# The last expert item: rows back to the tokens by one-hot matmuls, the other items' rows loaded while it runs

## What is computed

```python
def moe_swiglu(h, w_router, b_router, w_gate, w_up, w_down):
    ...
    logits = (t @ w_router).astype(jnp.float32)
    _, top_idx = lax.top_k(logits + b_router.astype(jnp.float32), TOP_K)      # 2 of 8 experts
    top_w = jax.nn.softmax(jnp.take_along_axis(logits, top_idx, axis=-1), axis=-1)
    gates = jnp.sum(jax.nn.one_hot(top_idx, N_EXPERTS) * top_w[..., None], axis=1)
    for e in range(N_EXPERTS):
        out = out + gates[:, e:e + 1] * swiglu(t, w_gate[e], w_up[e], w_down[e])  # 1024 -> 2816 -> 1024
...
y = rmsnorm(x + moe_swiglu(...), g_final)
```

## Time and profile before

| what | value |
|---|---|
| median of 3 runs | 1471.12 us (1465.41 to 1472.30) |
| profiled execution | 1469.05 us |
| its span, first to last instruction | 1467.2 us |
| mean granted TensorE clock | 0.965 of full speed |
| busy share: TensorE, VectorE, ScalarE, GpSimd | 94%, 64%, 52%, 5% |
| last matmul starts at | 1438.25 us of the span |

### The profile page before, as it was taken

One profiled execution on the slowest core, in us unless ns is written; L12 is line 12 of the kernel. 1 busy time (PEld: TensorE's weight loads), 2 busy tenths in 40 slices (PEclk: granted clock), 3 DMA queues, 4 the chain that ended last, 5 costly groups with the idle time before them and its releaser, 6 DMA issues.

```text
span 1467.2 us, 19059 instructions
## 1 busy us (share of the span) xinstructions
PE 1375.5 (94%) x6832; PEld 1109.2 (76%) x6832; DVE 933.8 (64%) x880; ACT 769.3 (52%) x742; POOL 73.7 (5%) x103
## 2 busy tenths in 40 slices
PE   4899999989989999968999999999999999999982
PEld 4789999877666555546888888888888888888871
DVE  2534343355445222237788888888888888888883
ACT  1433233334344222125777777777777777777761
POOL 1000000002100000000001001010010010100001
PEclk9899999999979999978999999999999999999996
DMA  8543443230212221276899999999999999999934
GB/s 260 187 157 106 167 130 127 79 132 11 65 35 84 84 65 45 78 288 258 324 365 366 399 362 378 380 362 395 360 371 386 373 385 364 373 391 362 382 116 125
DMA packets 136562, 354.98 MB, mean 242 GB/s; under 512 B 18282, under 2 KB 54458, under 8 KB 136177
## 3 DMA queue, kind: packets, MB, share of 16 engines
q1 hardware_dynamic: 133337, 343.73, 64.8%
q0 software_dynamic: 3184, 10.71, 1.9%
HBM read 346.74 MB, written 7.82 MB: 242 GB/s over the span
## 4 chain that ended last, share of the span: by engine, by line
PE 92%; DVE 3%; ACT 2%; DMA 1%; issue 1%; POOL 1%; SPq 0%; ACTq 0%; DVEq 0%; POOLq 0%
PE PS L1411 24%; PE PS L1413 23%; PE PS L1412 23%; PE PS L1684 3%; PE PS L1715 2%; PE PS L1752 2%; PE PS L1613 2%; PE PS L1717 1%; PE PS L1816 1%; PE PS L1425 1%; PE PS L1436 1%; PE PS L1577 1%; PE PS L1664 1%; PE PS L1587 1%; PE PS L1809 1%
## 5 line engine op out<-in xcount | busy, mean ns | idle before, releaser
L955 DVE TENSOR_TENSOR LOW<-RAW,UH 128x2048 fp32r<-128x2048 f32 x275 | 628.0, 2291 | 154.6 <-ACT UH L669 154.6
L669 ACT CAST UH<-RAW 128x2048 fp32r<-128x2048 f32 x275 | 526.1, 1914 | 253.5 <-PE PS L1413 253.5
L1411 PE MATMUL PS<-UH,XH 128*128 128x512 f32 (+1 forms) x768 | 292.5, 381 | 1.4 <-DVE XL L1308 1.4
L1412 PE MATMUL PS<-LOW,XH 128*128 128x512 f32 (+1 forms) x768 | 290.5, 378 | 0.0
L1413 PE MATMUL PS<-UH,XL 128*128 128x512 f32 (+1 forms) x768 | 290.5, 378 | 0.0
L1411 PEld LDWEIGHTS PS<-UH,XH 128*128 128x128 f32 x768 | 145.2, 189 | 30.5 <-DVE XL L1308 1.8
L1413 PEld LDWEIGHTS PS<-UH,XL 128*128 128x128 f32 x768 | 145.4, 189 | 29.3
L1412 PEld LDWEIGHTS PS<-LOW,XH 128*128 128x128 f32 x768 | 145.3, 189 | 28.5
L1411 PE MATMUL PS<-UH,ATH 128*128 128x512 f32 x352 | 138.4, 393 | 4.7 <-DVE ATL L1324 4.7
L1413 PE MATMUL PS<-UH,ATL 128*128 128x512 f32 x352 | 137.8, 392 | 0.0
L1412 PE MATMUL PS<-LOW,ATH 128*128 128x512 f32 x352 | 137.7, 391 | 0.0
(11 more groups left out here) (256 smaller groups left out, 1557.8 us busy)
## 6 DMA issues: line engine op xcount, KB each, us to landing
RAW<-in_moe_w_down SPq DMA_DIRECT2D x88, 1024.0 KB, 5.4
RAW<-in_moe_w_gate SPq DMA_DIRECT2D x64, 1024.0 KB, 5.1
RAW<-in_moe_w_up SPq DMA_DIRECT2D x64, 1024.0 KB, 5.1
RAW<-in_moe_w_gate SPq DMA_DIRECT2D x24, 768.0 KB, 6.5
RAW<-in_moe_w_up SPq DMA_DIRECT2D x24, 768.0 KB, 7.1
PAIR<-in_ffn_w_gate SPq DMA_DIRECT2D x11, 1024.0 KB, 5.2
PAIR<-in_ffn_w_up SPq DMA_DIRECT2D x11, 1024.0 KB, 7.8
RAW<-in_ffn_w_down SPq DMA_DIRECT2D x11, 1024.0 KB, 5.0
```

Source lines behind the costliest of these rows:

```text
L669: nc.scalar.copy(dst, src).then_inc(unit_high, 1)
L955: V_.tensor_tensor(dst, src, high.bitcast(F32), ALU.subtract).then_inc(unit_low, 1)
L1411: mm(out, wh, xh, start=start, stop=False, skip_group_check=True)
L1412: mm(out, wh, xl, start=False, stop=False, skip_group_check=True)
```

## The change

The rows of the last item no longer go through DRAM. Three one-hot tiles (BACK, slots x tokens of one tile) are made from the last item's column of IDX; the result is split into a high part (YH) and a low part (YL), and matmuls with BACK bring each row to its token, in free PSUM banks. VectorE adds them with the token's weight for that item (`RC[:, 4]`). The rows of the other items are loaded from YD as soon as ring slots 0 to 2 are free, and added with weights that are zero where a row belongs to the last item. As such rows in YD are now never written by an item, YD is filled with finite numbers early in the program. The last item's down of block 2 runs one output half after the other, and the turn of its hidden block stands one unit earlier. Empty slots now point at an extra row 0 of the tokens' buffer HND, so that they match no token. The table "items" is replaced by the start of "iota", and three semaphores of the gains become one.

```diff
+YG_FREE = next(i for i in range(len(LAST) - RING, len(LAST)) if (NF + i) % RING == 0) + 1   # 15
 ...
-    put("tokens", np.stack([token, token, 2 * token + 1, 2 * token + 2], 1))
+    put("tokens", np.stack([token + 1, token + 1, 2 * token + 1, 2 * token + 2], 1))
 ...
+    BACK = place("BACK", [P, NT, TT], F32R, XN_OFF)
+    YH = place("YH", [P, D], F32R, FFN_OFF + 3 * 4 * UNIT)
+    YL = place("YL", [P, D], F32R, FFN_OFF + 3 * 4 * UNIT + 4 * D)
 ...  SP
-        sp.wait_ge(y_last, 16)
         for t in range(NT):
+            sp.wait_ge(unit_used, NU * (before_last + 1) + NF + YG_FREE + t)
             rows = YD[1 + 2 * t * TT:1 + 2 * (t + 1) * TT, :].rearrange("(p i) d -> p (i d)", i=2)
             sp.dma_start(YG[t][:, :, :].rearrange("p i d -> p (i d)"), rows).then_inc(y_in[t], 16)
 ...  POOL, after the roots of the first dense layer
+        for t in range(NT):
+            pool.wait_ge(normed[1], t + 1)
+            for i in range(2):
+                store(YD[1 + 2 * t * TT:1 + 2 * (t + 1) * TT, :].rearrange("(p i) d -> p i d", i=2)[:, i, :], HN[:, t, :])
 ...
-                    pool.dma_start(HND[MIXED[k] * TT:(MIXED[k] + 1) * TT, :], HN[:, MIXED[k], :]).then_inc(y_stored, 16)
+                    if k == 0:
+                        pool.dma_start(HND[0:1, :], HN[0:1, MIXED[0], :]).then_inc(y_stored, 16)
+                    pool.dma_start(HND[1 + MIXED[k] * TT:1 + (MIXED[k] + 1) * TT, :], HN[:, MIXED[k], :]).then_inc(y_stored, 16)
 ...
+        nc.gpsimd.tensor_copy(IDXL[:, :], IDX[:, 0, :][:, bass.ds(before_last, 1)]).then_inc(back_ready, 1)
 ...  POOL, after the loop: the last item's scatter goes
-        pool.wait_ge(y_stored, 16 * before_last + 16 * NT)
-        pool.wait_ge(i_y, 2 * before_last + 4)
-        nc.gpsimd.tensor_copy(IDXY[:, :], IDX[:, 1, :][:, bass.ds(before_last, 1)]).then_inc(pool_step, 1)
-        steps[0] += 1
-        pool.wait_ge(pool_step, steps[0])
-        pool.indirect_dma_start(YD, bass.IndirectOffsetOnAxis(IDXY[:, 0:1], 0), YS[:, :], None).then_inc(y_last, 16)
 ...  ACT, item
+                if last and i == DN0:
+                    act.wait_ge(y_stored, 16 * j + 16 * (NT + 1))
 ...
-                elif i == GU0 - 1:
+                elif i == (GU0 - 2 if last else GU0 - 1):
                     hidden_high(2, j)
 ...
+            if last:
+                for h in range(2):
+                    act.wait_ge(unit_used, NU * (j + 1) + NF + len(order) - 2 + 2 * h)
+                    nc.scalar.copy(YH[:, h * 512:(h + 1) * 512], PS[:, 4 + h, :]).then_inc(i_y, 1)
+                return
 ...  DVE, before the second layer's first norm
+        dve.wait_ge(stored, 16 * (1 + 2 * NT))
 ...  DVE, item: hidden_low(2, j) moves as hidden_high does; after the last item
+        dve.wait_ge(back_ready, 1)
+        for t in range(NT):
+            V_.tensor_scalar(BACK[:, t, :], cn("iota")[:, 0:TT], float(1 + t * TT), IDXL[:, 0:1], ALU.add, ALU.is_equal)\
+              .then_inc(back_ready, 1)
         dve.wait_ge(r_act, 1)
         link(V_.tensor_tensor(rc(10), rc(6), rc(7), ALU.add))
         link(V_.reciprocal(rc(11), rc(10)))
         link(V_.tensor_tensor(RC[:, 6:8, :], RC[:, 6:8, :], RC[:, 11:12, :].to_broadcast([TT, 2, NT]), ALU.mult))
-        dve.wait_ge(gain4_in, 16)
+        link(V_.tensor_scalar(RC[:, 8:10, :].rearrange("p i t -> p (i t)"), SB[:, 0, :], TO[0:TT, 1, NE - 1:NE], -1.0,
+                              ALU.subtract, ALU.is_equal))
+        link(V_.tensor_tensor(RC[:, 0:2, :], RC[:, 6:8, :], RC[:, 8:10, :], ALU.mult))
+        link(V_.tensor_tensor(RC[:, 2:4, :], RC[:, 6:8, :], RC[:, 0:2, :], ALU.subtract))
+        link(V_.tensor_tensor(rc(4), rc(0), rc(1), ALU.add))
+        for t in range(NT):
+            dve.wait_ge(y_in[t], 16)
+            for i in range(2):
+                link(V_.scalar_tensor_tensor(out=X[:, t, :], in0=YG[t][:, i, :], scalar=RC[:, 2 + i, t:t + 1], in1=X[:, t, :],
+                                             op0=ALU.mult, op1=ALU.add))
+        for h in range(2):
+            dve.wait_ge(i_y, 2 * before_last + 3 + h)
+            cols = slice(h * 512, h * 512 + 512)
+            V_.tensor_tensor(YL[:, cols], PS[:, 4 + h, :], YH[:, cols].bitcast(F32), ALU.subtract).then_inc(back_ready, 1)
+        dve.wait_ge(later_gain_in, 48)
 
         def add_rows(t):
-            dve.wait_ge(y_in[t], 16)
-            link(V_.scalar_tensor_tensor(out=X[:, t, :], in0=YG[t][:, 0, :], scalar=RC[:, 6, t:t + 1], in1=X[:, t, :],
-                                         op0=ALU.mult, op1=ALU.add))
-            V_.scalar_tensor_tensor(out=X[:, t, :], in0=YG[t][:, 1, :], scalar=RC[:, 7, t:t + 1], in1=X[:, t, :],
-                                    op0=ALU.mult, op1=ALU.add).then_inc(x_added, 1)
+            dve.wait_ge(back_mm, t + 1)
+            V_.scalar_tensor_tensor(out=X[:, t, :], in0=PS[0:TT, back_bank(t):back_bank(t) + 2, :].rearrange("p b n -> p (b n)"),
+                                    scalar=RC[:, 4, t:t + 1], in1=X[:, t, :], op0=ALU.mult, op1=ALU.add).then_inc(x_added, 1)
 ...  PE, item
-            units(j, order, DN1, GU0)
+            units(j, order, DN1, GU0 - 1 if last else GU0)
 ...
             turn_hidden(2, j)
+            units(j, order, GU0 - 1 if last else GU0, DN2 if not last else GU0)
+            pe.wait_ge(i_atl, 6 * j + 6)
 ...
+            pe.wait_ge(unit_low, NU * (j + 1) + NF + len(LAST))
+            for h in range(2):
+                for q in range(3):
+                    slot, high = (NF + GU0 + q) % RING, (NF + GU0 + q) % HIGH
+                    for i in range(2):
+                        cols = slice((2 * i + h) * 512, (2 * i + h + 1) * 512)
+                        ins = three(PS[:, 4 + h, :], ATH[:, 2 * q + i, :], ATL[:, 2 * q + i, :], UH[high][:, cols],
+                                    LOWS[slot][:, cols], False, q == 2 and i == 1)
+                ins.then_inc(unit_used, 1 + h)
 ...  PE, after the last item
+        pe.wait_ge(back_ready, 1 + NT)
+        for t in range(NT):
+            for h in range(2):
+                if t == 0:
+                    pe.wait_ge(back_ready, 1 + NT + h + 1)
+                cols = slice(h * 512, h * 512 + 512)
+                mm(PS[0:TT, back_bank(t) + h, :], BACK[:, t, :], YH[:, cols], start=True, stop=False, skip_group_check=True)
+                ins = mm(PS[0:TT, back_bank(t) + h, :], BACK[:, t, :], YL[:, cols], start=False, stop=True, skip_group_check=True)
+            ins.then_inc(back_mm, 1)
+def back_bank(t):
+    return (0, 2, 6)[t]
```

More of the change, by code:

```diff
@@ L112, in landed @@
     return every, here + (1 if slot < NF else 0)
+YG_FREE = next(i for i in range(len(LAST) - RING, len(LAST)) if (NF + i) % RING == 0) + 1
+assert YG_FREE + 4 <= len(LAST)
 KB = [(0, 128), (128, 128), (256, 16)]
@@ L125 @@
 _W = [("ident", 128), ("upper", TT), ("iota", 128), ("part", 1), ("mask", 2 * P), ("maskt", TP), ("maskd", NS),
-      ("cos", NT * HALF), ("sin", NT * HALF), ("ridx", NE), ("tri", NE * NE), ("steps", NE * NT), ("items", MAXI), ("slots", MAXI + 2), ("tokens", 4 * NT)]
+      ("cos", NT * HALF), ("sin", NT * HALF), ("ridx", NE), ("tri", NE * NE), ("steps", NE * NT), ("slots", MAXI + 2), ("tokens", 4 * NT)]
 _WP = [("pm0", 4 * P), ("pm1", 4 * P), ("pstate", 4 * SMP)]
@@ L162, in shape_constants @@
     put("steps", np.tile(steps.reshape(1, -1), (P, 1)))
-    put("items", np.tile(np.arange(MAXI), (P, 1)))
     put("slots", np.tile(CAP * np.arange(MAXI + 2), (P, 1)))
     token = TT * np.arange(NT)[None] + np.arange(P)[:, None]
-    put("tokens", np.stack([token, token, 2 * token + 1, 2 * token + 2], 1))
+    put("tokens", np.stack([token + 1, token + 1, 2 * token + 1, 2 * token + 2], 1))
     def band(a, b, w):
@@ L319, in program @@
     EG = get("EG", [P, 1024])
+    XN_OFF = get.cur[0]
     XN = get("XN", [P, D])
@@ L363, in program @@
     x_in, consts_in, gains_in = sem("x_in"), sem("consts_in"), sem("gains_in")
-    gain1_in, gain4_in, small_in = sem("gain1_in"), sem("gain4_in"), sem("small_in")
-    gain3_in, dense_done = sem("gain3_in"), sem("dense_done")
+    later_gain_in, small_in = sem("later_gain_in"), sem("small_in")
+    dense_done = sem("dense_done")
     gain0_in, pool_in, pool_w_in = sem("gain0_in"), sem("pool_in"), sem("pool_w_in")
@@ L420, in program @@
         sem(n) for n in ("i_idx", "i_ix", "i_iy", "i_xn", "i_xt", "i_xh", "i_xl", "i_sg", "i_a", "i_t", "i_ath", "i_atl", "i_y", "y_stored"))
-    y_last = sem("y_last")
+    back_ready, back_mm = sem("back_ready"), sem("back_mm")
     y_in = [sem(f"y_in{t}") for t in range(NT)]
@@ L490, in _ @@
         sp.wait_ge(x_pooled, NT)
-        sp.dma_start(G[0][:, :], a["g_mix"][1:2, :].partition_broadcast(TT)).then_inc(gain1_in, 16)
+        sp.dma_start(G[0][:, :], a["g_mix"][1:2, :].partition_broadcast(TT)).then_inc(later_gain_in, 16)
         for c in range(RING_D, NC):
@@ L642, in _ @@
             pool.indirect_dma_start(XN[:, :], None, HND[:, :], bass.IndirectOffsetOnAxis(IDXC[:, 0:1], 0)).then_inc(i_xn, 16)
```

(20 more changed lines are left out.)

11 lines of the change are left out of this document (6 added, 5 removed).

## The result

| | before | after |
|---|---|---|
| median | 1471.12 us (1465.41 to 1472.30, 3 runs) | 1459.27 us (1457.84 to 1460.88, 4 runs) |
| profiled execution | 1469.05 us | 1457.84 us |
| its span | 1467.2 us | 1456.2 us |
| first to last index copy of the loop (six items) | 569.67 us | 570.72 us |
| last index copy to the end of the span | 103.67 us | 91.35 us |

The ratio of the mean times is 0.993, with an interval of 0.9906 to 0.9955: faster by 7 to 14 us. The median of 1459.27 lies within the 1450 to 1463 that was predicted, 2.8 above the 1456.5 named. The upper end of the interval lies just short of the 0.5% that can be told from no change. One disturbed run of the kernel before (1769.95) is left out.

A forecast was written before the change was run, and what follows sets the result against it. Bound taken: the 28.5 us tail after the last matmul, each step waiting for the previous. Savings of 5.3 (copy, scatter), 6.0 (load), 0.2 (stop) and 2.1 (adds) make 13.6: span 1453.6, predicted time 1456.5, range 1450 to 1463.

The forecast's parts named there:

- Scatter and load leave the path: In the tail: copy and scatter of the last item's rows save 5.3 us, the load of expert rows 6.0.
- The loads are hidden: Other items' rows, loaded after units 14 to 16, land by about 1419 us, 11 us before they are needed.
- The start of the down: The last down projection starts at 1428.36 us instead of 1428.60, a gain of 0.24.
- The 10.06 us of the down: The last down's 36 matmuls take 10.06 us as before, with the same loss of clock, ending at 1438.42.
- VectorE's new work: Under the last down: one-hot tiles 0.85 us, small operations 1.4, six adds 7.9, ending at 1438.4, tied with TensorE.
- The add out of PSUM: One add per tile in the tail, read from PSUM, takes 1.28 us, as the add of before.
- The root: GpSimd's root ahead of the first normalisation takes 0.9 us; 2.5 if slowness came from first use.
- At no cost: Six early 448 KB stores, the extra token row, index column copy, constants and merged semaphores add no time.
- Half clock to the end: Rival: TensorE stays at half clock from the last down to its end; 1461.7 to 1463.8 us, chance 0.09.
- Loads not hidden: Rival: other items' rows land only after the last down; gain only 1 to 2 us, 1468, chance 0.05.
- VectorE late: Rival: dearer VectorE work under the last down plus a slow root cost 3 to 4 us, 1460; within the main case.
- Starved dense steps: Rival: early stores hold back the first dense steps' weights, lasting until about 83 us at worst; slower, chance 0.03.

The follow-up runs named there:

- late_loads: Changed kernel with the loads of the other items' rows issued after the last down projection; last index copy to end 107.2 us, against 91.35 in the changed kernel.
- filled_stop: Changed kernel with 36 unneeded turns of the identity on TensorE in the stop ahead of the last down; last index copy to end 90.0 us, against 91.35.
- after_old_addresses: Changed kernel with 13 unused columns in the constants, so later tiles lie where they did before; median 1457.25 us, ratio to the kernel before 0.9906.
- stores_four_times: Changed kernel with the early stores into the expert rows made four times (24 instead of 6); span 1456.8 us, against 1456.2.
- tail_reordered: Changed kernel with old addresses, waits per unit, small operations ahead of the loop, reordered adds, back matmuls by halves; median 1451.54 us, ratio to the kernel before 0.9884.
- wait_per_unit: Changed kernel whose last down's first half waits for each weight unit's low part alone; median 1458.33 us, ratio to the kernel before 0.9934.

## Why the prediction was right, step by step

**Scatter and load leave the path: right.** The add of the first tile starts 2.2 us after the last down matmul, and no DMA stands in the chain until the outputs.

**The loads are hidden: right.** Landed by about 1418.5 (forecast 1419); late_loads shows what the cover is worth, 15.8 us.

**The start of the down: right.** 1429.65, where 1428.36 was forecast. The cast of unit 23 before it is already 1.39 late (1421.98 instead of 1420.59); without that the forecast is met to 0.1. The turn now takes place at 1421.78, between the two units.

**The 10.06 us of the down: mis-sized.** It was taken over from before, "the same loss of clock"; 13 slow matmuls instead of 9 made it 11.25, 1.2 more. That a stop costs the clock was right, as filled_stop shows; but a granted clock of 0.5 beyond the first nine matmuls is one of the prediction's own signs of being wrong, and the six adds end 1.5 us ahead of the last down matmul, not within the microsecond that it asked for. With the old addresses the down takes 10.12 (after_old_addresses), so the term was carried over from one set of addresses to another; what joins addresses and clock stays open.

**VectorE's new work: right.** One-hot tiles 0.65 instead of 0.85, small operations and adds as forecast; the adds end at 1439.43, and 1438.4 with the delay of 1.39 is 1439.8. The forecast named the tie as its weakest number, rightly: either engine alone gives 0 to 1.35 us, both 2.8. That a clock that does not fall would give nothing holds only where the two tie: it gave 1.35 in filled_stop, and after_old_addresses, whose down takes 10.12, ends as early as filled_stop (90.1 and 90.0).

**The add out of PSUM: right.** 1.28, as an add with both inputs in SBUF (1.28, L1405). The fixed part that the Trainium skill states as larger out of PSUM (VectorE: DVE Perf Modes, the section on the TRN2 errata) isn't seen in these rows.

**The root: right.** 0.9 and not 2.5. The second pair shows the reason: 1.06 where it starts under a normalisation, which reads two tensors in SBUF (1446.60 to 1447.88), and 0.57 for the next operation under the add out of PSUM; in tail_reordered 1.20 under an add of two SBUF inputs (1442.39 to 1443.67), after 73 us without work. That is the lock of the Trainium skill (SBUF — State Buffer, section "SBUF: two separate sides"); all rows here agree, and the rival of first use falls.

**"At no cost": wrong in one word, the constants.** The stores cost nothing, as stores_four_times shows. But the constants without the table of items move every tile behind them by 64 bytes, and the items become 0.17 us longer, 1.05 between the copies. The 1.2 us of the down go with the same addresses. The prediction counted the instructions of that edit and not the addresses.

So 1.39 us upstream (1.05 in the loop by the addresses, 0.27 ahead of its first copy, 0.07 in the last item) and 1.2 of clock make the 2.6 that the gain fell short, and in these profiles all but the 0.27 goes with the addresses; everything behind the second low row took 13.97 us (1442.23 to 1456.2) where 13.85 were forecast.

**The rivals.** Half clock to the end: no, it returned after 13 matmuls. Loads not hidden: no, but its price in late_loads is higher than worked out. VectorE late: no, TensorE was. Starved dense steps: no, not with four times the stores.

## What to carry to other kernels

Where two engines run side by side into one point, cost both, and expect of an edit to either one no more than the distance between them; here 0 and 1.35 alone, 2.8 together. Read a small change from a milestone near it, since the part ahead of it can vary by more than the change. When taking a table out of (or into) a block of constants, keep the addresses of what lies behind it, or time the loop with both.

## What the runs showed of the chip

- A shift of all later tiles by 64 bytes changes an item of 94.95 us to 95.12, in both directions: 94.95 in the four profiles with the old addresses, 95.12 in the nine with the new. Behind a stop of 4.3 to 4.7 us the last down takes 10.1 us in the three profiles with the old addresses and 11.1 to 11.4 in the six with the new. The cause inside the chip stays open for both.
- The granted clock stood at about 0.5 after each stop of 4.3 to 4.7 us here (for 8 to 14 matmuls, 3.4 to 6 us, the fewer with the old addresses) and stayed at 1.00 over the stops of 1.95 to 2.3 us in wait_per_unit, filled_stop and tail_reordered. Work that nobody needs, small turns of the identity, keeps it up as well.
- After the stops ahead of the back matmuls, 16.0 us in late_loads and 4.64 in wait_per_unit, these run at the lower clock too, and the first add behind them waits 1.67 and 1.68 us instead of 0.88.
